# Second-layer expert blocks rounded, split and multiplied in column halves, and row gathers issued three blocks sooner

## The reference

```python
def peer_ffn(x, wq, subkeys, u, v):
    # q = x @ wq; product keys pick, per token and head, 16 of the 128*128 experts
    ...
    def chunk(args):
        xc, ec, gc = args
        hid = jax.nn.gelu(jnp.einsum('cd,chkd->chk', xc, u[ec]))
        return jnp.einsum('chk,chkd->cd', gc * hid, v[ec])
    ...
```

## Time and profile before

| | |
|---|---|
| median of 3 runs | 2014.98 us (2013.48 to 2015.31) |
| the profiled execution | 2022.3 us, its span 2020.5 us |
| TensorE (PE) busy | 1931.2 us, 96% of the span |
| VectorE (DVE), ScalarE (ACT), POOL busy | 59%, 31%, 10% |
| moved over the span | 538.46 MB, mean 266 GB/s |
| mean granted TensorE clock | 0.983 |

### The profile page before, as it was taken

One profiled execution on the slowest core, in us unless ns is written; L12 is line 12 of the kernel. 1 busy time (PEld: TensorE's weight loads), 2 busy tenths in 40 slices (PEclk: granted clock), 3 DMA queues, 4 the chain that ended last, 5 costly groups with the idle time before them and its releaser, 6 DMA issues.

```text
span 2020.5 us, 28973 instructions
## 1 busy us (share of the span) xinstructions
PE 1931.2 (96%) x11574; PEld 1721.7 (85%) x11574; DVE 1195.1 (59%) x1781; ACT 620.3 (31%) x784; POOL 192.4 (10%) x148
## 2 busy tenths in 40 slices
PE   8999999998999998999899989999999998999997
PEld 7979999898999998999876667689999996666765
DVE  5424665566348287777367768843233336778775
ACT  5223445444330101111233434420000003444444
POOL 0000000000000011121111101111221111101110
PEclk9999999998999999999999999999999999999999
DMA  6655443455535697899967878879899897788874
GB/s 239 217 219 179 137 145 125 169 175 180 186 125 180 229 334 293 294 356 355 362 229 288 325 281 306 315 293 378 341 342 363 339 368 295 302 314 320 307 287 167
DMA packets 79196, 538.46 MB, mean 266 GB/s; under 512 B 8652, under 2 KB 11980, under 8 KB 18061
## 3 DMA queue, kind: packets, MB, share of 16 engines
q1 hardware_dynamic: 57068, 386.33, 52.6%
q0 software_dynamic: 22048, 151.07, 19.0%
HBM read 516.85 MB, written 20.45 MB: 266 GB/s over the span
## 4 chain that ended last, share of the span: by engine, by line
PE 49%; issue 33%; DVE 6%; POOL 5%; DMA 4%; ACT 3%; POOLq 0%; SPq 0%; DVEq 0%; ACTq 0%
PE bank L814 13%; PE bank L530 7%; PE bank L531 7%; PE bank L532 7%; POOL rows_sb L496 5%; PE bank L868 2%; DVE lo L1622 2%; ACT hi L1180 2%; DMA rows_sb<-in_u_rows,pairs 2%; PE bank L619 1%; PE bank L899 1%; PE bank L900 1%; PE bank L905 1%; PE bank L907 1%; PE bank L906 1%
## 5 line engine op out<-in xcount | busy, mean ns | idle before, releaser
L814 PE MATMUL bank<-hT,raw 128*128 128x192 f32 x4096 | 673.6, 327 | 1.3 <-ACT kept L1190 1.3
L814 PEld LDWEIGHTS bank<-hT,raw 128*128 128x128 f32 x4096 | 668.0, 191 | 2.0 <-issue 2.0
L1622 DVE TENSOR_TENSOR lo<-raw,hi 128x2048 fp32r<-128x2048 f32 x128 | 293.1, 2289 | 162.0 <-ACT hi L1180 161.8
L530 PE MATMUL bank<-act,hi 128*128 128x256 f32 x1216 | 354.6, 292 | 11.1 <-DVE act L1219 6.9
L531 PE MATMUL bank<-act,hi 128*128 128x256 f32 x1216 | 347.5, 286 | 0.0
L532 PE MATMUL bank<-act,lo 128*128 128x256 f32 x1216 | 347.3, 286 | 0.0
L1180 ACT ACTIVATE hi<-raw 128x2048 fp32r<-128x2048 f32 x128 | 245.2, 1916 | 324.8 <-PE bank L907 324.8
L1211 DVE TENSOR_TENSOR lo<-raw,hi 128x2048 fp32r<-128x2048 f32 x76 | 174.1, 2291 | 146.7 <-ACT hi L950 84.1
L899 PE MATMUL bank<-hi,wm 128*128 128x512 f32 x512 | 211.6, 413 | 50.8 <-DVE wm L1626 42.3
L530 PEld LDWEIGHTS bank<-act,hi 128*128 128x128 f32 x1216 | 236.8, 195 | 20.1 <-issue 19.4
L531 PEld LDWEIGHTS bank<-act,hi 128*128 128x128 f32 x1216 | 237.1, 195 | 1.6 <-issue 1.4
(11 more groups left out here) (248 smaller groups left out, 1623.8 us busy)
## 6 DMA issues: line engine op xcount, KB each, us to landing
raw<-in_u SPq DMA_DIRECT2D x128, 1024.0 KB, 6.6
raw<-in_v SPq DMA_DIRECT2D x128, 1024.0 KB, 6.2
raw<-in_w_in SPq DMA_DIRECT2D x44, 1024.0 KB, 5.2
raw<-in_w_out SPq DMA_DIRECT2D x16, 1024.0 KB, 5.3
raw<-in_wq SPq DMA_DIRECT2D x16, 1024.0 KB, 4.9
gate_matrix<-gs POOLq DMA_DIRECT2D x12, 1024.0 KB, 7.7
gs<-gate_matrix SPq DMA_DIRECT2D x16, 768.0 KB, 8.1
raw<-in_cmp_w SPq DMA_DIRECT2D x8, 1024.0 KB, 4.9
```

What stands on the lines that cost most here:

```text
L530: mm(dst, wh, mh, start=first, stop=False)
L814: last = mm(bank[s % 2][:, 0:TD], raw[:, s, k * P:(k + 1) * P], xn[:, k, 0:TD], start=(k == 0), stop=(k == KT - 1))
L1622: vec.tensor_tensor(lo[:, mv % 2, :], raw[:, mv % RAW, :], hi[:, mv % 2, :].bitcast(F32), ALU.subtract).then_inc(lo_ready, 1)
```

## The change

Four things are changed. First, in the v stages each rounding (L1180) and each subtraction (L1622) is split into two of 1024 columns, each with a signal on new semaphores, `v_hi_ready` and `v_lo_ready`. Second, a block of TensorE waits for the first halves, works on column groups 0 and 1 for both token tiles, signals `v_half_done`, waits for the second halves and works on column groups 2 and 3; the last block of each half keeps the old order of matmuls. From the third block on, ScalarE's first half waits for `v_half_done` instead of `block_done`. Third, SP's refills of `raw` behind v blocks wait for the second half's `v_lo_ready`. Fourth, POOL's wait before a gather names a block that is three earlier (`GATHER_LEAD`), in all stages.

```diff
--- before.py
+++ after.py
@@ -55,7 +55,7 @@
...
-def m_split(half): return M_PEER + HALF * half
+def v_halves(half): return 2 * HALF * half
...
@@ -67,6 +67,7 @@
...
 FIRST_GATHERS = 12
+GATHER_LEAD = 3
...
@@ -320,6 +321,7 @@
...
             sem(s) for s in ("dots_ready", "hcol_ready", "wcol_ready", "acc_step", "res_added", "half_stored", "half_loaded"))
+        v_hi_ready, v_lo_ready, v_half_done = (sem(s) for s in ("v_hi_ready", "v_lo_ready", "v_half_done"))
         fold_ready, folded, fin_added = (sem(s) for s in ("fold_ready", "folded", "fin_added"))
...
@@ -417,9 +419,17 @@
...
+            def load_after_v(src, done, s):
+                sp.wait_ge(v_lo_ready, done)
+                sp.dma_start(raw[:, s, :], src).then_inc(raw_loaded[s], 16)
             for half in range(2):
                 for s in range(RAW):
-                    load_after(a["u"][HALF * half + s], m_split(half) - RAW + s, s)
+                    if half:
+                        load_after_v(a["u"][HALF + s], 2 * (HALF - RAW + s) + 2, s)
+                    else:
+                        load_after(a["u"][s], M_PEER - RAW + s, s)
                 with sp.Fori(1, HALF // RAW) as lap:
...
@@ -428,7 +438,7 @@
...
                     else:
-                        load_after(a["v"][:, mv + HALF * half, :], mv + (m_split(half) - RAW), s)
+                        load_after_v(a["v"][:, mv + HALF * half, :], 2 * mv + (v_halves(half) - 2 * RAW + 2), s)
...
@@ -516,7 +526,7 @@
...
                 if ahead:
-                    pool.wait_ge(block_done, M_PEER + b - 1)
+                    pool.wait_ge(block_done, M_PEER + b - 1 - GATHER_LEAD)
                 for i in ahead:
...
@@ -888,25 +898,43 @@
...
-                    pe.wait_ge(hi_ready, mv + (m_split(half) + 1))
-                    pe.wait_ge(lo_ready, mv + (m_split(half) + 1))
                     pe.wait_ge(wm_hi, mv + (HALF * half + 1))
...
                     whole, packed, rest = w[:, 0:P], w[:, P:2 * P], w[:, 2 * P:3 * P]
-                    for dc in range(4):
+                    def split_loaded(part):
+                        pe.wait_ge(v_hi_ready, 2 * mv + (v_halves(half) + 1 + part))
+                        pe.wait_ge(v_lo_ready, 2 * mv + (v_halves(half) + 1 + part))
+                    def second_tile(dc):
                         cols = slice(dc * 512, (dc + 1) * 512)
                         mm(bank[4 + dc][:, :], packed, vh[:, cols], start=opening, stop=False, skip_group_check=True)
-                        last = mm(bank[4 + dc][0:TS, :], packed[:, 0:TS], vl[:, cols], start=False, stop=closing, skip_group_check=True)
-                        if closing:
-                            last.then_inc(sums_done, 1)
-                    for dc in range(4):
+                        return mm(bank[4 + dc][0:TS, :], packed[:, 0:TS], vl[:, cols], start=False, stop=closing, skip_group_check=True)
+                    def first_tile(dc):
                         cols = slice(dc * 512, (dc + 1) * 512)
...
                         mm(bank[dc][:, :], whole, vh[:, cols], start=False, stop=False, skip_group_check=True)
-                        last = mm(bank[dc][:, :], rest, vh[:, cols], start=False, stop=closing, skip_group_check=True)
-                        if closing and dc < 3:
-                            last.then_inc(sums_done, 1)
+                        return mm(bank[dc][:, :], rest, vh[:, cols], start=False, stop=closing, skip_group_check=True)
+                    if closing:
+                        for dc in range(4):
+                            if dc % 2 == 0:
+                                split_loaded(dc // 2)
+                            second_tile(dc).then_inc(sums_done, 1)
+                        for dc in range(4):
+                            last = first_tile(dc)
+                            if dc < 3:
+                                last.then_inc(sums_done, 1)
+                    else:
+                        for dc in range(4):
+                            if dc % 2 == 0:
+                                split_loaded(dc // 2)
+                            second_tile(dc)
+                            last = first_tile(dc)
+                            if dc == 1:
+                                last.then_inc(v_half_done, 1)
                     last.then_inc(block_done, 1)
...
@@ -1176,8 +1204,15 @@
...
                     ac.wait_ge(raw_loaded[s], 16 * (n // RAW + 1))
-                    ac.wait_ge(block_done, m_v(half) + mv - 1)
-                    do(hi[:, s % 2, :], raw[:, s, :], ACT.Copy).then_inc(hi_ready, 1)
+                    for part in range(2):
+                        if mv < 2:
+                            ac.wait_ge(block_done, m_v(half) + mv - 1)
+                        elif part == 0:
+                            ac.wait_ge(v_half_done, (HALF - 1) * half + mv - 1)
+                        else:
+                            ac.wait_ge(block_done, m_v(half) + mv - 1)
+                        cols = slice(part * 1024, (part + 1) * 1024)
+                        do(hi[:, s % 2, cols], raw[:, s, cols], ACT.Copy).then_inc(v_hi_ready, 1)
...
@@ -1617,9 +1652,11 @@
...
                                       ALU.mult).then_inc(gated, 1)
-                    split = m_split(half) + mv
-                    dv.wait_ge(hi_ready, split + 1)
-                    vec.tensor_tensor(lo[:, mv % 2, :], raw[:, mv % RAW, :], hi[:, mv % 2, :].bitcast(F32), ALU.subtract).then_inc(lo_ready, 1)
+                    for part in range(2):
+                        cols = slice(part * 1024, (part + 1) * 1024)
+                        dv.wait_ge(v_hi_ready, v_halves(half) + 2 * mv + part + 1)
+                        vec.tensor_tensor(lo[:, mv % 2, cols], raw[:, mv % RAW, cols], hi[:, mv % 2, cols].bitcast(F32),
+                                          ALU.subtract).then_inc(v_lo_ready, 1)
                     dv.wait_ge(wm_hi, mv + (HALF * half + 1))
...
```

## The result

The changed kernel takes **1954.14 us** in the median of 4 runs (1952.46 to 1954.79); the kernel before, on the same chip, 2014.23 (2011.79 to 2015.31, 4 runs). The ratio is 0.9692, with an interval of 0.9673 to 0.9711. The prediction said 1953.

The account below looks back on a forecast made before the run. TensorE was taken to be paced in the v stages by the rounding-subtraction chain and late rows; 61.5 + 4.3 - 1.3 = 64.5 us off the profiled 2022.3 gives 1957.8; median taken as 1953, between 1950.5 and 1957; range 1943 to 1976.

Parts of the forecast that it names:

- The v stages: Both v stages: 70.7 us lost to waits, less 5.2 half clock, 1 gelus, 3 uneven rows, so 61.5 us gained.
- Floor: TensorE in the v stages: a block of 20 matmuls that does not wait lasts 4.58 us.
- Rows that land unevenly: Gathered rows in the v stages: 3 us of the loss stays because of uneven landings.
- Gelu places: Five v-stage places where the gelu stands behind a gathered row: each 0.2 us late, 1 us in all.
- Half clock at the entries: TensorE at the start of both v stages: half clock stays, 5.2 us of loss not recovered.
- Prices of the pieces: Halves of 1024 columns in v blocks: 1.06 us for a rounding on ScalarE, 1.22 for a subtraction on VectorE.
- Waits in the middle of a block: TensorE's extra waits and signal at the half boundary of v blocks: cost nothing; far bound 0.33 each, 42 us.
- The rival with this price: Waits inside v blocks hold back TensorE's weight loads: 1995 us at 0.33 each, 2030 at 0.6; chance 0.06.
- Before the v stages: Routing stop of TensorE at L858 and its half clock go: 2.6 + 1.7 = 4.3 us gained.
- Against it: Losses of 0.5 us at half 0's entry and 1.5 at the second u stage, 0.7 gained at half 1's; net -1.3.
- Memory takes over: Rival: in the v stages late loads give back 10 to 20 us, 1963 to 1973 us; chance 0.16.
- The lead eaten: Rival: POOL behind a buffer or store, v-stage rows late, 28 us plus 5 of half clock, 1986 us; chance 0.07.

Follow-up runs that it names:

- old_order: The changed kernel with first halves of roundings also waiting for the end of block n-2, and every block's matmuls in the old order; 1970.26 us.
- waits_first: The changed kernel with all of TensorE's waits moved to the start of a block; 1954.09 us.
- after_again: The changed kernel measured once more, with no edit, as the base of a later group; 1953.68 us.
- lead_late: The changed kernel with the lead of three blocks only for gathers from the first v stage on, earlier ones as before; 1957.55 us.
- lead_none: The changed kernel with gathers let go as before (lead 0 instead of 3 blocks), so the halves alone; 2021.63 us.
- port_sbuf: The changed kernel plus unused VectorE additions, both operands in SBUF, beside 24 gathered rows of the second u stage; 1954.5 us.
- lead_only: The kernel before with gathers let go three blocks sooner and nothing else; 2004.02 us.
- port_psum: The changed kernel plus the same unused VectorE additions as port_sbuf, but one operand of each in a PSUM bank; 1954.03 us.

## Why the prediction was right, point by point

**The total.** From profiled execution to profiled execution the change took 2022.3 - 1953.6 = 68.7 us; the sum said 64.5. The medians differ by 60.1. The prediction had to choose between 1950.5 (the 7.3 us from the profiled time to the median are a constant) and 1957 (they are stops). The changed kernel's profiled execution lies 0.6 below its median, and the kernel before spreads over 16 us: no constant, its profiled execution was one of the longer ones. The three runs that the prediction started from, 2014.98, were on the low side: the later groups have 2017.8 to 2019.9, and 64.5 off these is 1953.3 to 1955.4. So the sum was right, and that the middle of two readings of the 7.3 us came within 1.2 us of the result is luck. What makes that kernel spread was not tried; the changed one spreads over 2.3 us.

**The v stages.** They lost 33.7 and 28.8 us, 62.5 together, against 61.5. Chain and lead were right. What remains of the loss is 8.2 us, where 9.2 was forecast, and that is partly luck: the floor was 4 us too low, rows and half clock 5 too high.
- Floor 4.58 a block: 4.61 was measured, 0.03 x 128 = 4 us more. The old order brings 4.58 back (old_order), moving the waits does not (waits_first). The prediction counted matmuls and weight loads, and these are the same; the new order, which goes back and forth between the two token tiles, costs 0.03 a block.
- Rows that land unevenly: 3 us taken, 0 measured. The list of VectorE's waits in both stages has none for a row.
- Gelu places: 0.2 each taken, 0.2 measured: the block with the gelu lasts 4.72 (its successor starts 0.11 late), the next one, with its slow first matmul, 4.70.
- Half clock at the entries: 5.2 us taken as lost; half 0's window at 0.50 has 3.3 us inside the stage, half 1's 3.2, and half of these 6.5 is lost, 3.3.
- Prices of the pieces: 1.06 and 1.22 us held. ScalarE is busy 20.3 us more in the two stages and VectorE 12.3, where the rows had said 26 and 9. By *Perfetto Trace Analysis*, section *Optimizing Scalar/DVE Operations*, of the Trainium skill, which has about 93 ns an instruction on ScalarE and 60 on VectorE, the prediction had estimated 12 and 8; over the stages the trace lies between on ScalarE and above both on VectorE. Where two halves follow each other without a pause the page's figures hold: 1.99 us for both on ScalarE against 1.90 for a whole rounding, 2.35 against 2.29 for a subtraction.

**Readings that were wrong without harm.** "Even an undisturbed turn loses 0.40": the chain of 4.98 us is as read, but undisturbed blocks last 4.98 and 4.66 in turn, so only about every second one waits, as the 36 and 35 waits of the earlier trace rows say. The sum goes by the stages' totals and is not touched. The 5.7/8.5/15.9 of the earlier trace rows were taken for the v stages, but that view runs on over the second u stage; in the v stages alone the landings are 5.7/8.0/11.4 and 5.9/8.6/11.0. 351 GB/s at 0.92 make 382, not 390, and the low end of the range comes to 1944 to 1945, not 1943.

**Waits in the middle of a block** at nothing: shown by waits_first, 0.4 us apart from after_again. The rival with this price falls.

**Before the v stages**: 4.3 forecast for the routing stop and its half clock; both went. A second stretch of half clock, at the one-hots, became 3.4 us instead of 6.8 too, 1.7 us that the prediction had not looked for. lead_late gives 3.9 for the earlier gathers up to there, but only 0.5 of the 2.60 us stop came back in it.

**Against it**: half 0's entry waits 6.03 us instead of 5.27 (a loss of 0.5 was forecast; after_again's has 4.50, so it varies by more than that), half 1's 4.40 instead of 4.97 (a gain of 0.7 was forecast). The burst of two rows at the second u stage, forecast at -1.5, cost nothing: TensorE waits once in that stage, 1.3 us for the half sums, as in the kernel before.

```profile
PE bank L824 <- ACT kept L1225: 1.3, 1, 1.3
```

The terms add up: 62.5 in the v stages, 5.7 ahead of them (2.6 + 1.7 + 1.7 - 0.8, and 0.5 that is not accounted for), 0.6 at half 1's entry: 68.8, against 68.7 measured.

**Memory takes over**: no. 322 and 316 GB/s were moved, close to the 329 and 320 worked out, and no wait of TensorE, VectorE or ScalarE in the v stages was put down to a transfer.

**The lead eaten**: this did not happen, but lead_none shows what it would have been, and the price was far too low: 2021.6, not 1986. It had 28 us of stops and three stretches of half clock; lead_none's profiled execution has 51 us of stops inside the v stages and ten stretches. Three things were off. VectorE wants a row sooner than was reckoned: 9.47 us after its issue began in the earlier trace rows, 7.03 with halves, which is 2.4 sooner and not 1.5. The loss does not come from the median landing, which in lead_none is 7.9 and 7.5 us, but from the late ones, of up to 14.8. And the landings are not independent of the halves, since the gather's issue on POOL can take 5.5 us instead of 0.94. The changed kernel shows it too. In half 0's v stage the issues and landings are, before and after,

```profile
L496 POOL DMA_INDIRECT rows_sb<-in_v,pairs x13: 936/1165/2902, 1002.9 to 1328.9; - x13
L496 POOL DMA_INDIRECT rows_sb<-in_u_rows,pairs x12: 938/1164/2912, 1038.8 to 1291.4; - x12
...
DMA to landing us min/median/max: 5.7/8.0/11.4
```

```profile
L506 POOL DMA_INDIRECT rows_sb<-in_v,pairs x12: 936/1292/5563, 996.3 to 1276.9; - x12
L506 POOL DMA_INDIRECT rows_sb<-in_u_rows,pairs x12: 1294/3168/5552, 1006.3 to 1244.4; - x12
...
DMA to landing us min/median/max: 5.5/10.2/15.1
```

The issue of 1115.00 ends 0.81 after VectorE's unbroken stretch of two-operand work does (1119.73), when it first waits:

```profile
1115.00 5.54 POOL L506 DMA_INDIRECT rows_sb<-in_u_rows,pairs  x1 [8.28 <-PE bank L919]
```

That the halves lengthen the issue because VectorE works in longer unbroken stretches is read from such timelines and not shown: in port_sbuf POOL also got in during a stretch. What is shown is that the longest issue in a v stage is 2.9 us before, 3.5 in lead_only and 5.6 with halves, and that in the port pair two operands in SBUF are what holds it.

With three blocks of lead this costs nothing. *SBUF — State Buffer*, section *Who interferes with whom*, of the Trainium skill has a rule that fits: a VectorE operation with two inputs in SBUF contends with a GpSimd instruction that reads SBUF, over a port pair that the two share, and one with at most one input there does not, outside VectorE's 2-port modes. The pair port_sbuf and port_psum agrees, 7.06 us against 0.93. The same section infers that such an operation does not hold up the making of a DMA's descriptors; it did lengthen this gather's issue. That it is the gather's reading of its indices that waits was not tried.

So the two parts were rightly forecast as a pair and wrongly weighed apart: the prediction gave the lead the long stops and the halves the 0.40 a turn, as if one could be had without the other. The halves make rows wanted sooner and let some land later; only the lead makes them worth anything.

## What to carry to other kernels

Before two edits are priced one by one, ask whether the first makes the second's problem worse: here an engine that got faster wanted its prefetched rows 2.4 us sooner and, with both operands in SBUF, held their issue up by as much as 4.6, and the 50 us of one edit existed only after the other. Measure a prefetch by the spread of its landings, not by the median, and give it the longest one with room to spare (two blocks of 4.6 us were enough, one was not). Where a chain is longer than the block it hides behind, let the next stage's first piece go when the first piece of the buffer is free; waits already satisfied in the middle of TensorE's stream cost nothing measurable here (waits_first, 0.4 us), so they can be put where they release earliest.

## What the hardware showed that was not expected

- POOL's issue of an indirect gather takes 0.94 us undisturbed and up to 5.57 us (7.06 in port_sbuf) beside VectorE work on operands that are both in SBUF, though not each time; with one operand in PSUM it takes 0.93 or 0.94 beside the same work.
- Twenty matmuls of 512 columns take 4.61 us when they change between the two token tiles, and so between two banks, in every column group, and 4.57 to 4.58 with all of one tile first.
